# A three-network fp32 kernel on one core: the two exponentials of an attention period move ahead of the second and the third group of casts on ScalarE

## What is computed

```python
# first block: branch a (banded, bias by relative position) and branch b (top-k mask), 4 heads each
sc = einsum('bcqhd,bckhd->bhcqk', qc, kb) * d ** -0.5 + bias;  p = softmax(sc);  o = einsum(p, vb)
# even layer, second attention: difference of two softmaxes over 1024 + 256 keys, 4 heads of 128
a = p[:, :, 0] - lam * p[:, :, 1];  yb = rmsnorm(einsum('bhqk,bkhe->bqhe', a, v))
# odd layer: neighbourhood attention, 8 heads, window of 8 rows (512 keys, with bias) + 256 context keys
# odd layer: attention with q = [nope 128, rope 64], 4 heads, 1024 + 256 keys, values of 128
p = softmax(einsum('bqhd,bkhd->bhqk', q, k) * q.shape[-1] ** -0.5);  o = einsum('bhqk,bkhe->bqhe', p, v)
```

## Time and profile before

| | |
|---|---|
| runs | 4438.46, 4439.7, 4455.2 us; median 4439.7 |
| profiled execution | 4450.23 us, its span 4448.4 us, mean granted TensorE clock 0.908 |
| TensorE busy | 3732.5 us, 84% |
| VectorE, ScalarE busy | 2302.6 us (52%), 1457.9 us (33%) |
| GpSimd busy, DMA | 296.2 us (7%), 230 MB moved, mean 52 GB/s |

### The profile page before, as it was taken

How to read it: one execution, slowest core, us unless ns; L and a number is a source line. 1 busy time by engine, 2 the same in 40 slices (tenths; PEclk the granted TensorE clock), 3 DMA queues, 4 the chain that set the end, 5 groups by cost and what they waited for, 6 DMA issues and landing times. The chain is left out here.

```text
span 4448.4 us, 44928 instructions
## 1 busy us (share of the span) xinstructions
PE 3732.5 (84%) x18492; PEld 2963.7 (67%) x18492; DVE 2302.6 (52%) x3898; ACT 1457.9 (33%) x2559; POOL 296.2 (7%) x379
## 2 busy tenths in 40 slices
PE   3799987786989999998888787776968888788887
PEld 2688875665767888886666676665847777555556
DVE  4899345655743222224466465666346565334444
ACT  3221143444122111113353344444134444222331
POOL 2121100001100000000100000000010000000000
PEclk9899968887989999998899899997979999878888
DMA  2133231001411111112100100001210000000011
GB/s 81 34 123 119 104 137 35 25 19 60 183 56 36 52 50 48 48 48 71 39 21 32 31 29 26 25 30 42 86 65 33 29 32 34 18 15 9 24 52 66
DMA packets 69292, 229.97 MB, mean 52 GB/s; under 512 B 8472, under 2 KB 12568, under 8 KB 69088
## 3 DMA queue, kind: packets, MB, share of 16 engines
q1 hardware_dynamic: 43056, 132.68, 8.9%
q0 software_dynamic: 22576, 81.85, 5.3%
q10 hardware_dynamic: 3456, 12.58, 0.7%
HBM read 180.42 MB, written 36.17 MB: 49 GB/s over the span
## 5 line engine op out<-in xcount | busy, mean ns | idle before, releaser
L2126 PE MATMUL PS<-m,m 128*128 128x512 f32 (+2 forms) x3560 | 1421.6, 400 | 284.6 <-DVE m L2470 54.6
L2127 PE MATMUL PS<-m,m 128*128 128x512 f32 (+2 forms) x3560 | 1381.8, 389 | 0.0
L2128 PE MATMUL PS<-m,m 128*128 128x512 f32 (+2 forms) x3560 | 1380.7, 388 | 0.0
L2126 PEld LDWEIGHTS PS<-m,m 128*128 128x128 f32 (+1 forms) x3560 | 689.9, 194 | 481.2 <-issue 112.3
L2128 PEld LDWEIGHTS PS<-m,m 128*128 128x128 f32 (+1 forms) x3560 | 689.7, 194 | 136.3
L2127 PEld LDWEIGHTS PS<-m,m 128*128 128x128 f32 (+1 forms) x3560 | 692.1, 195 | 120.8 <-issue 2.7
L2216 PE MATMUL PS<-m,m 64*128 64x256 f32 (+5 forms) x1968 | 374.7, 412 | 86.1 <-ACT m L2386 59.5
L2470 DVE TENSOR_TENSOR m<-m,m 128x1024 fp32r<-128x1024 f32 (+4 forms) x203 | 207.8, 1024 | 415.5 <-ACT m L2303 414.8
L2397 ACT CAST m<-PS 128x512 fp32r<-128x512 f32 x352 | 205.7, 589 | 595.6 <-PE PS L2225 594.0
L2216 PEld LDWEIGHTS PS<-m,m 64*128 64x128 f32 (+1 forms) x1968 | 240.8, 208 | 225.8 <-issue 127.1
L2755 DVE TENSOR_TENSOR m<-PS,m 128x512 fp32r<-128x512 f32 x352 | 240.9, 689 | 287.9 <-ACT m L2397 287.0
(11 more groups left out here) (203 smaller groups left out, 3911.9 us busy)
## 6 DMA issues: line engine op xcount, KB each, us to landing
m<-in_w SPq DMA_DIRECT2D x220, 512.0 KB, 3.3
g_scratch<-m ACTq DMA_DIRECT2D x24, 512.0 KB, 2.8
m<-g_scratch POOLq DMA_DIRECT2D x24, 512.0 KB, 4.7
m<-in_w SPq DMA_DIRECT2D x32, 256.0 KB, 2.6
x_scratch<-m POOLq DMA_DIRECT2D x2, 4096.0 KB, 12.4
m<-m POOLq DMA_DIRECT2D x60, 128.0 KB, 2.7
y_scratch<-m POOLq DMA_DIRECT2D x12, 512.0 KB, 2.9
m<-y_scratch POOLq DMA_DIRECT2D x12, 512.0 KB, 5.3
```

The costliest lines, as they stand in the source:

```text
L2126: pe.e.engine.matmul(o, L[0], X[0], start=start, stop=False)
L2127: pe.e.engine.matmul(o, L[0], X[1], start=False, stop=False)
L2128: return pe.e.engine.matmul(o, L[1], X[0], start=False, stop=stop)
```

## The change

```diff
@@ -534,11 +534,10 @@
                     if fill:
                         fill.drain()
                     u["scored"](f1["n"])
-                pull(0.5)
-                turn()
-                pull(0.7)
+                pull(0.35)
                 self.soft2(f0)
                 turn()
+                pull(0.6)
                 self.soft2(f1)
                 while turns:
                     turn()
```

## The result

The changed kernel takes 4471.5 us (median of 6 runs, 4463.9 to 4475.7), the kernel before on the same chip 4441.3 us (6 runs, 4438.5 to 4455.2). The ratio is 1.0062, its 95% interval 1.0046 to 1.0078: slower by 0.6%, some 28 to 30 us. The forecast was 4470. The profiled execution has a span of 4473.9 us, 25.5 more than the one of before.

What follows compares the result with a forecast made beforehand. The prediction took TensorE, busy 84% of the span, as where time is won or lost. Its terms, 12 + 3 + 2 + 4 + 12 - 4 - 5 + 6 = +30 us on 4439.7, gave 4470 us, range 4430 to 4505.

Steps and rivals of the forecast that it cites:

- the loads (87): Sign named for the whole kernel: 87 table loads in place of 71.
- the stall of 2 us and more: Sign in a three-turn period of the difference attention: the third turn waits 2 us or more for a subtraction.
- the copy behind two exponentials: Sign in the difference attention: a fill-bank copy stands behind two exponentials, TensorE waiting 3 to 4 us once a head.
- a, stall at the turn bank: Difference attention: second cast moves behind the first exponential, so TensorE stands 2.4 us at the third turn; period +1.8 us.
- b, copy behind the second exponential: Difference attention, one period on: fill-bank copy comes behind exponential, cast, exponential, so the scores start 2.3 us later.
- c, what takes it back: Difference attention: later waits swallow delays, leaving about 4 us a head; +12 for three heads, +3 for the fourth.
- d, table loads: 16 added loads of 1.28 us: +2 at difference attention's head starts, +4 in the first block.
- e, last attention: Last attention's 16 periods: products wait for a delayed cast, +1.1 us in nine periods without fill; +12 us in all.
- f, where it helps: Neighbourhood attention and first block: exponentials with early bounds start sooner, nothing stands on the delayed cast; -4 and -5 us.
- g, clock: New idle times cool TensorE: one more cold period in the last attention, a few half-cold in the difference attention; +6 us.
- gain: Rival: scores wait for the second exponential, so earlier exponentials cut waits and stalls stay hidden; 4400 us, chance 0.16.
- clock: Rival: new 2.5 us waits drop the clock in most of the last attention's nine clean periods; 4503 us, chance 0.08.

Runs made afterwards that it cites:

- moved: Kernel before with only the exponentials moved forward in all four attentions, fill shares kept at 0.5 and 0.7: 4443.4 us against 4442.8, ratio 1.0007.
- shares: Kernel before with only the fill shares changed to 0.35 and 0.6 in all four attentions, exponentials in their old places: 4433.8 us against 4442.8, ratio 0.9989.
- loads: Kernel before with the new order in first block and difference attention, except where no turn is left (first block: also one-turn periods): 4472.1 us against 4442.8, ratio 1.0075.
- last: Kernel before with the new order in the last attention only: 4454.2 us against 4447.0, ratio 1.0025.

## Why the prediction was right, and where it was not

The time (4470 for 4471.5) and the side were right. The stall at the turn bank and the late copy were right, in the stretch that decided. But most terms were mis-sized, and that the total fits within 2 us is luck: the profiled kernel is 14 us worse than forecast in the difference attention and 5 in the neighbourhood, 13 us better in the first block and 7 in the last attention. Of the signs named beforehand, the loads (87), the stall of 2 us and more, the copy behind two exponentials (3.5 us, though in two heads of four) and the wait of over 2 us in the last attention came; the sizes did not: the difference attention grew by 30.7 instead of 15 to 25, the last one by 4.6 instead of 10 to 20, and the neighbourhood grew by 1.3 instead of shrinking.

- **a, stall at the turn bank:** right. Forecast 2.4 us of standing and +1.8 for the period; measured 2.13, and 14.0 us against 12.2. *moved*, where TensorE's order is that of before and turns wait 29.3 us for the bank instead of 10.8, shows that the moved exponentials cause it.
- **b, copy behind the second exponential:** right in kind; +3.3 us instead of +2.3. The copy ended 3.9 us after the bound, as worked out (4.0), but the three steps behind it took 3.3 us instead of 2.1, with matmuls of 0.63 us instead of 0.39 from 1 us behind a wait of 3.54 us on.
- **c, what takes it back:** too generous. I ended 4 us late per head; the periods with turns of the first three heads lost 18.3 us, 6.1 each. The take-backs are there mainly in a head's last two long periods (-0.8 and -1.4 us in the third head). The fourth head lost 3.3, forecast 3. I carried the rule at full clock and did not see that shares and exponentials together cost more than their sum.
- **d, table loads:** in the first block the periods ahead of new heads lost 3.3, 0.4 and 0.9 us, near the +4, but that loads cost it is not shown: the first of them lasts 27.4 us before, 30.7 in the changed kernel and 30.4 in *shares*, where no exponential moved, but 27.0 in *moved*, which has two more loads in it. In the difference attention the heads' starts lost 9 instead of 2, of which *loads* ties about 5 to the order in periods without turns; that the loads themselves cost it is not shown (see *loads*). TensorE waits 10.3 us more for the squares (L2310) there, but 9.5 less for VectorE's L2510, and in *loads* both are back within 0.1 us. What the other half is stays open; the clock is lower in it. ScalarE's busy time grew by 21.8 us, near the 20.5 of sixteen loads.
- **e, last attention:** +12 forecast, +4.6 in the profile. The nine profiled executions with the old order there took 365.2 to 390.1 us (mean 378.3), the three with exponentials moved forward 381.0 to 394.7 (mean 388.9), 10.6 more; the ranges overlap, but *last* by itself is slower (+7.2 us, ratio at least 1.0013). The wait was right, its price per clean period 2.5 instead of 1.1, with the lower clock in it, and periods elsewhere happened to be less cold.
- **f, where it helps:** the first block's gain was mis-sized, -13.8 for forecast -5 + 4: I read the waits of whole stretches, not the two periods that became 10.5 us shorter. Three heads of the neighbourhood gave -4.2 as forecast; the fourth, from which I took the row, lost 5.5. There "nothing stands on the delayed cast" was wrong: VectorE's subtraction stands on it, and the next bound behind that.
- **g, clock:** not one more cold period but half-cold ones where the new waits stand. In the difference attention TensorE's busy time grew by 8.9 us; in the last one it fell by 10.3 and in the first block by 5.3, and over the whole kernel it stayed the same (3732.5 and 3731.4 us). So +6 was too little for the stretch with the new waits, and too much for the whole.

Of the rivals, *gain* names what happens in the first block and in the neighbourhood's fill heads, *clock* what happens in the last attention's clean periods, where a wait of 2.67 us stands in a period with a granted clock of 0.86 instead of 1.00. The Trainium skill, "TensorE: Matmul & The Clock Gate" (section "HAM oscillation"), describes a kernel whose TensorE waits 3 to 5 us for a transfer in each step of its loop and starts the next burst at the lower clock every time. The traces agree in kind, with shorter waits, and add that one and the same wait of 2.57 us did it in one kernel and not in another.

## What to carry to other kernels

An in-order engine should not be given a waiting instruction ahead of one that is ready: moving an exponential forward paid where its bound was already there, and cost where ScalarE then stood for the bound with a cast behind it that frees the only bank. It also cost with two banks, where VectorE's next bound came behind the subtraction that waits for the delayed cast and no fill covered it. So an order written once for several loops is best judged loop by loop, and even head by head; here the same edit gave -14, +31, -4 and +5 us. And a forecast that lands on the total has not shown its terms: cut both traces at the same places before believing it.

## What the runs showed of the hardware

The last attention's stretch took from 365.2 to 390.1 us with one and the same order of instructions, in nine profiled executions of kernels that differ only ahead of it; its share of cold periods (granted clock 0.83 to 0.92 over the stretch) goes with it. The times fall into groups: 383.4 to 383.9 in four kernels, 365.2 in two. Two profiled stretches before and after a change can thus differ by 25 us without a cause in the change. Whether the time of arrival decides, or how much one and the same kernel varies there from execution to execution, was not tested.
